# Expert stage of a two-block kernel: plain column halves with eight 64-wide turnings, an earlier position table, a later modulation slot and a split last load

## The reference, cut to what matters

```python
g_p, g_idx = lax.top_k(group_prob, 1)                 # one of 4 groups
e_p, e_idx = lax.top_k(jax.nn.softmax(sel, axis=-1), 2)  # two of its 8 experts
expert = g_idx * EXPERTS_PER_GROUP + e_idx            # 32 experts in all
...
def expert_block(args):                               # xbk: the expert's tokens
    xbk, e = args
    return (jax.nn.silu(xbk @ w_gate[e]) * (xbk @ w_up[e])) @ w_down[e]
...
y = jnp.zeros((N + 1, D)).at[tok_buf].add(yb * w_buf[:, None])
```

## Time and profile before

| | us |
|---|---|
| median of 3 runs | 1467.42 |
| profiled execution | 1468.59 |
| its span | 1466.7 |
| TensorE busy with MATMUL | 1418.4 (97%) |
| first window of expert 0 begins | 256.60 |
| last expert's down product ends | 706.01 |
| one window, from a down product to the next | 13.39 |

### The profile page before, as it was taken

One profiled execution on the slowest core, in us unless ns is written; L12 is line 12 of the kernel. 1 busy time (PEld: TensorE's weight loads), 2 busy tenths in 40 slices (PEclk: granted clock), 3 DMA queues, 4 the chain that ended last, 5 costly groups with the idle time before them and its releaser, 6 DMA issues.

```text
span 1466.7 us, 23746 instructions
## 1 busy us (share of the span) xinstructions
PE 1418.4 (97%) x9490; PEld 930.3 (63%) x9491; DVE 630.2 (43%) x1120; ACT 230.2 (16%) x473; POOL 220.3 (15%) x156
## 2 busy tenths in 40 slices
PE   6999999999999999999999999999999999999997
PEld 4766756654544444444585649998448664999943
DVE  1455646112122222221463425557665472555666
ACT  1320004100000000000312531001031052200001
POOL 2000100000000000000000027770010002677101
PEclk9999999999999999999999999999999999999999
DMA  9954297999999999999999155345428923352610
GB/s 351 330 224 173 91 414 301 368 389 424 417 426 429 427 427 427 428 426 427 407 408 361 69 197 205 117 168 205 172 103 343 379 93 115 104 184 85 232 56 29
DMA packets 91074, 400.92 MB, mean 273 GB/s; under 512 B 7248, under 2 KB 12496, under 8 KB 67824
## 3 DMA queue, kind: packets, MB, share of 16 engines
q1 hardware_dynamic: 90992, 399.73, 69.2%
HBM read 398.66 MB, written 1.05 MB: 273 GB/s over the span
## 4 chain that ended last, share of the span: by engine, by line
PE 88%; DVE 4%; DMA 4%; ACT 1%; issue 1%; SPq 1%; DVEq 0%; ACTq 0%
PE psum L1168 22%; PE psum L1521 17%; PE psum L1573 8%; PE psum L1333 8%; PE psum L1146 4%; PE psum L1483 4%; PE psum L726 3%; DMA ring<-in_moe_up 3%; PE psum L1351 2%; PE psum L1553 2%; PE psum L1366 2%; PE psum L648 1%; DMA ring<-in_ada_w 1%; PE psum L882 1%; PE psum L1114 1%
## 5 line engine op out<-in xcount | busy, mean ns | idle before, releaser
L1168 PE MATMUL psum<-ring,arena 128*64 128x256 f32 (+1 forms) x1728 | 241.1, 433 | 6.1 <-issue 3.8
L1168 PEld LDWEIGHTS psum<-ring,arena 128*64 128x64 f32 x1728 | 123.9, 136 | 126.9 <-issue 70.0
L1521 PE MATMUL psum<-arena,ring 128*128 128x128 f32 x1280 | 150.4, 275 | 2.1 <-ACT arena L2371 2.0
L1521 PEld LDWEIGHTS psum<-arena,ring 128*128 128x128 f32 x1280 | 146.4, 192 | 2.8 <-issue 2.8
L1168 PE MATMUL psum<-arena 128*64 128x256 f32 (+1 forms) x812 | 112.6, 429 | 2.4 <-issue 1.7
L1521 PE MATMUL psum<-arena 128*128 128x128 f32 x960 | 113.7, 275 | 0.0
L1333 PE MATMUL psum<-arena,ring 128*128 128x256 f32 x512 | 112.0, 380 | 1.5 <-DVE arena L1632 1.5
L1521 PEld LDWEIGHTS psum<-arena 128*128 128x128 f32 x960 | 110.4, 192 | 0.0
L1997 DVE TENSOR_TENSOR arena<-psum,arena 128x256 f32<-128x256 f32 x32 | 13.6, 425 | 222.4 <-PE psum L1168 222.4
L1333 PEld LDWEIGHTS psum<-arena,ring 128*128 128x128 f32 x512 | 96.8, 190 | 16.6 <-issue 2.7
L1573 PE MATMUL psum<-arena 128*128 128x512 f32 x220 | 99.3, 593 | 2.1 <-DVE arena L2307 2.1
(11 more groups left out here) (444 smaller groups left out, 1768.8 us busy)
## 6 DMA issues: line engine op xcount, KB each, us to landing
ring<-in_moe_up SPq DMA_DIRECT2D x22, 2048.0 KB, 17.7
ring<-in_moe_down SPq DMA_DIRECT2D x22, 2048.0 KB, 17.1
ring<-in_moe_gate SPq DMA_DIRECT2D x21, 2048.0 KB, 17.5
arena<-in_w_mod SPq DMA_DIRECT2D x32, 1024.0 KB, 8.5
ring<-in_ada_w SPq DMA_DIRECT2D x12, 2048.0 KB, 10.9
ring<-in_w_qkv SPq DMA_DIRECT2D x12, 2048.0 KB, 15.0
arena<-in_moe_gate SPq DMA_DIRECT2D x20, 1024.0 KB, 16.6
arena<-in_moe_up SPq DMA_DIRECT2D x20, 1024.0 KB, 16.2
```

Of the source, the lines that this page charges most:

```text
L1168: ins = mm(bank[b][o, 0:n], lhsT, part_of(w, half), start=first, stop=last, tile_position=(0, 64 * half))
L1521: last = mm(bank[b + k][:, slot * P:slot * P + P], left[:, k, c], right[:, c, :], start=(c == 0), stop=(c == 3))
```

## The change

Seven edits, in the order of the program:

- **Plain columns.** `hidden` is gone: half 0 of gate and up is hidden columns 0 to 255, half 1 is 256 to 511, read without gaps.
- **Turning.** Since the halves lie otherwise, `actm` is turned by eight products with a piece of the identity, each 64x64, in the two column halves of TensorE; their stationary operand is every fourth column of `actm`. `actT` has four chunks of 64 columns.
- **Tokens by chunk.** ScalarE writes the normalized tokens so that the 128 features of a chunk lie side by side; `gather` then reads its stationary operand without gaps, and ScalarE reads its input with a step of 8 elements (L2485 and L2491 of before).
- **Positions.** One of the two `rows` products now stands ahead of the five position products, the other behind; `fill(1)` stands behind both instead of ahead, and the flush behind the first half of `gather`. The ring slot that `fill(1)` reads is freed by the first `gather`, not by the first position product. VectorE's work on the experts' weights stands behind `perm`, and `spread4` behind `mtab`. On ScalarE the modulation copy stands behind the two `gate2b` copies.
- **Loop.** 8 passes in the loop; the ninth is written out, on SyncE and TensorE.
- **Last load.** The last `w_down` comes in two loads of 1 MB, with a semaphore each; TensorE waits for the second ahead of its third chunk.

The diff, cut to its core:

```diff
@@ sync: loads @@
-                at_e = bass.ds(i * PASS + e, 1) if e >= FIRST else slice(e, e + 1)
+                at_e = slice(NE - 1, NE) if last else bass.ds(i * PASS + e, 1) if e >= FIRST else slice(e, e + 1)
+                    if last:
+                        for h in range(2):
+                            sp.dma_start(ring[:, r, 2048 * h:2048 * h + 2048], rows_of[:, h, :])\
+                                .then_inc(S(("once_in", f"slot{r}_loaded")[h == 0]), 16)
+                        return
@@ tensor: between choice and experts @@
-            fill(1)
+            rows(diag[:, 1], 2, 3, parts=(0,))
 
             pe.wait_ge(S("routed"), 4)
-            mm(bank[6][:, 0:NE], upper[:, :], oh[:, 0], start=True, stop=True).then_inc(S("slot_freed"), 1)
+            mm(bank[6][:, 0:NE], upper[:, :], oh[:, 0], start=True, stop=True)
...
-            rows(diag[:, 1], 2, 3)
-            flush()
+            rows(diag[:, 1], 2, 3, parts=(1,))
+            fill(1)
...
-                return mm(gathered(half, c), xr[:, t, :].rearrange("q (p c) -> q c p", c=DC)[:, c, :],
+                return mm(gathered(half, c), xr[:, t, P * c:P * c + P],
                           perm[:, t, TOK * half:TOK * half + TOK], start=(t == 0), stop=(t == 1))
...
-                gather(0, c, 0)
+                ins = gather(0, c, 0)
+                if c == 0:
+                    ins.then_inc(S("slot_freed"), 1)
...
+            flush()
             pe.wait_ge(S("routes_ready"), 1)
@@ tensor: window @@
-                def hidden(w, half):
-                    return w.rearrange("p (q h j) -> p h q j", h=2, j=2)[:, half]
-                def columns(w, half):
-                    return w[:, 512 * half:512 * half + 512]
-                        ins = mm(bank[b][o, 0:n], lhsT, part_of(w, half), start=first, stop=last,
+                        ins = mm(bank[b][o, 0:n], lhsT, w[:, half * n:(half + 1) * n], start=first, stop=last,
                                  tile_position=(0, 64 * half))
...
-                for j in range(2):
-                    last = nc.tensor.transpose(bank[1][:, TOK + j * P:TOK + (j + 1) * P],
-                                               actm.rearrange("p (q j) -> p j q", j=2)[:, j, :], ident[:, :])
+                for k in range(4):
+                    for half in range(2):
+                        hs = slice(64 * half, 64 * half + 64)
+                        last = mm(bank[1][hs, TOK + 64 * k:TOK + 64 * k + 64], actm.rearrange("p (q k) -> p k q", k=4)[:, k, :],
+                                  ident[:, hs], start=True, stop=True, tile_position=(0, 64 * half))
...
-                    last = product(3, actT[:, k % 2, 64 * (k // 2):64 * (k // 2) + 64], w(k), 512, k == 0, k == 3, columns)
+                    last = product(3, actT[:, k, :], w(k), 512, k == 0, k == 3)
...
-            with pe.Fori(0, (NE - FIRST) // PASS, 1) as i:
+            with pe.Fori(0, PASSES - 1, 1) as i:
                 for e in range(FIRST, FIRST + PASS):
                     expert(i, e)
+            for e in range(FIRST, FIRST + PASS):
+                expert(PASSES - 1, e, e == FIRST + PASS - 1)
@@ scalar: normalized tokens, both halves of the tokens @@
-            a_.to(A(xr[:, 0, :], x[:, 0, :], ACT.Copy, scale=stat[:, 2:3]), "h2_ready")
+            a_.to(A(by_chunk(xr[:, 0, :]), x[:, 0, :].rearrange("q (p c) -> q c p", c=DC), ACT.Copy, scale=stat[:, 2:3]), "h2_ready")
```

More of the change, by code:

```diff
@@ L354, in _, with load_matrix @@
             moe_n0 = st_sp.n
-            def load_matrix(i, e, k, halves=(0, 1)):
-                at_e = bass.ds(i * PASS + e, 1) if e >= FIRST else slice(e, e + 1)
+            def load_matrix(i, e, k, halves=(0, 1), last=False):
+                at_e = slice(NE - 1, NE) if last else bass.ds(i * PASS + e, 1) if e >= FIRST else slice(e, e + 1)
                 one = a[("moe_gate", "moe_up", "moe_down")[k]][at_e, :, :]
@@ L403, in _ @@
                 load_matrix(0, *divmod(n, 3))
-            with sp.Fori(0, (NE - FIRST) // PASS, 1) as i:
+            with sp.Fori(0, PASSES - 1, 1) as i:
                 for e in range(FIRST, FIRST + PASS):
@@ L407, in _ @@
                         load_matrix(i, e, k)
+            for e in range(FIRST, FIRST + PASS):
+                for k in range(3):
+                    load_matrix(PASSES - 1, e, k, last=(e == FIRST + PASS - 1 and k == 2))
             st_sp.n += 11 * RING - 1
@@ L1026, in _, with rows @@
                     .then_inc(S("gn_var"), 1)
-            def rows(src, n, b0, freed=None):
+            def rows(src, n, b0, freed=None, parts=(0, 1)):
                 pe.wait_ge(S("diag_ready"), n)
@@ L1031, in rows @@
                     pe.wait_ge(S(freed[0]), freed[1])
-                for k in range(2):
+                for k in parts:
                     mm(bank[b0 + k][:, :], ones[:, :], src[:, 4 * k:4 * k + 4, :], start=True, stop=True)\
@@ L1154, in window, with product @@
             def window(slots, done, frees, copies):
[L1157 to L1165 removed]
+                def product(b, lhsT, w, n, first, last):
                     for half in range(2):
                         o = slice(64 * half, 64 * half + 64)
[L1168 removed]
+                        ins = mm(bank[b][o, 0:n], lhsT, w[:, half * n:(half + 1) * n], start=first, stop=last,
                                  tile_position=(0, 64 * half))
@@ L1197, in window, with expert, second_half @@
                 for k in range(4):
-                    last = product(3, actT[:, k % 2, 64 * (k // 2):64 * (k // 2) + 64], w(k), 512, k == 0, k == 3, columns)
+                    last = product(3, actT[:, k, :], w(k), 512, k == 0, k == 3)
                 last.then_inc(S("down_done"), 1)
-            def expert(i, e):
+            def expert(i, e, last=False):
                 def entry(n):
                     return mtab[0:1, bass.ds(i * PASS + n, 1)] if e >= FIRST else mtab[0:1, n:n + 1]
+                def second_half(w, c):
+                    if c == 2:
+                        pe.wait_ge(S("once_in"), 112)
+                    return w[:, c, :]
                 extra = pe.value_load(entry(NE + e), min_val=0, max_val=3) if e else extra0
@@ L1220, in slots @@
                         w = ring[:, r, :].rearrange("p (c n) -> p c n", c=chunks)
+                        if last and k == 2:
+                            return lambda c: second_half(w, c)
                         return lambda c: w[:, c, :]
@@ L1952, in _ @@
                                                 op0=ALU.is_equal, op1=ALU.add), "perm_ready")
+            dve.wait_ge(S("g_sum"), 2)
+            d(V.reciprocal(gs, gs))
+            dve.wait_ge(S("g_sum"), 3)
+            d(V.tensor_scalar(p1, dd, 1.0, None, ALU.add))
+            d(V.reciprocal(p1, p1))
+            d(V.tensor_tensor(w1, gs, p1, ALU.mult))
             d(V.tensor_tensor(w2, w1, dd, ALU.mult))
-            d.to(V.tensor_tensor(spread4.rearrange("p t k q -> p (t k) q"), ident[:, :].unsqueeze(1).broadcast_to([P, 8, P]),
-                                 vals.rearrange("p t k -> p (t k)").unsqueeze(2).broadcast_to([P, 8, P]), ALU.mult),
-                 "routes_ready")
             dve.wait_ge(S("iota_made"), 2)
@@ L1977, in _ @@
             d.to(V.tensor_copy(mtab[0:1, 2 * NE:3 * NE], pa[0:1, :]), "mtab_ready")
+            d.to(V.tensor_tensor(spread4.rearrange("p t k q -> p (t k) q"), ident[:, :].unsqueeze(1).broadcast_to([P, 8, P]),
+                                 vals.rearrange("p t k -> p (t k)").unsqueeze(2).broadcast_to([P, 8, P]), ALU.mult),
+                 "routes_ready")
             mod_columns()
```

15 lines of the change are left out of this document (6 added, 9 removed).

## The result

The changed kernel takes 1481.73 us (median of five runs, 1476.29 to 1484.91) against 1466.89 for the kernel before: a ratio of 1.0087, with a 95% interval of 1.0065 to 1.0110. It is slower, as forecast, but by 14.8 us where 6.6 were forecast. The profiled execution is the fastest of the five: 1476.29 us with a span of 1474.3. That is 1.1 us over the 1475.2 that the sum gave for a profiled execution; the median is 7.7 us over the forecast of 1474.0 and lies outside the forecast's own range of 1470.3 to 1480. So there are two questions: whether each step holds in the profiled execution, and what the other executions have on top.

The account below looks back on a forecast made before the run. TensorE bounds the expert stage until expert 28, then the loads. From the profiled 1468.59 us: +10.2 windows, -3.5 waits, -0.8 gather, +0.7 stalls = +6.6, so 1475.2, or 1474.0 as median; own range 1470.3 to 1480, 8 in 10 1465.5 to 1484.

Parts of the forecast that it names:

- The bound: Expert stage: TensorE sets the time until expert 28, the loads behind it; longer windows paid nearly in full, 32 times.
- Plain columns, -0.35: Gate and up products: reading columns without gaps saves 0.35 us per window, bounds 0 and 0.5.
- Rival 3: Gate and up: plain columns save nothing, a window grows by 0.67 us, time 1485; chance 0.08.
- The turning, 1.11: Turning of actm in each window: eight products take 1.11 us instead of 0.44, bounds 0.6 and 2.1.
- Rivals 1 and 4: Turning: 1, cheap, kernel faster, 1465.9 at 0.6 us, chance 0.15; 4, halves' loads follow one another, 2.1 us, 1506, chance 0.07.
- rival 1: Turning is cheap and the kernel gets faster; edge at a turning of 0.92 us, 115 ns a pair; chance 0.15.
- Waits for up matrices, -3.5: Last three experts: TensorE's 3.5 us of waits for up matrices go, since TensorE is now the later one.
- Second gather, -0.8: Second half of gather: plain operand saves 0.8 us that counts; the first half's is lost in a pause.
- Positions and loads, 0: Before the first window: it starts at 256.6 as before, within 0.4; two loads some 2.9 us later cost 0.
- Last load in halves, 0: Last down matrix in two loads: gains 0, since the up matrix was what came late.
- Stalls of fresh code, +0.7: Written-out ninth pass: +2.0 for 1.1 stalls of 1.8 us, -1.3 for low clock gone; bounds -6.7 and +7.

Follow-up runs that it names:

- second profile: Profiled execution of a repeat of the unaltered changed kernel, 1482.89 us; that repeat's median was 1482.64 us, ratio 1.0094 to the kernel before.
- window alone: Kernel before with only the plain column halves and the eight 64x64 turnings: 1478.8 us, ratio 1.0081.
- The one with 8 KB pieces: Kernel before with plain gate and up columns, its two transposes kept, down matrix in two 8 KB pieces a partition: 1466.8 us, ratio 0.9998.

## Why the prediction was right, and where it was off

**The bound.** Right. TensorE and the loads are two chains of nearly the same length, and the stage ends with the later. All windows tried show it: 13.71 us and no wait for a matrix; 13.39 and three last windows of some 14.7; 13.05 and eight of 14.8; 12.98 and eleven of 14.9. A longer window is paid 32 times, a shorter one brought nothing in any of the five versions that had one.

**Plain columns, -0.35.** Measured -0.34 (10.83 to 10.49), in every kernel that has them. Rival 3 falls by this. The rule of the Trainium skill (SBUF — State Buffer, the note on cachelines), by which two hits in a line are enough for full bandwidth and nothing would be saved, does not hold exactly for this moving operand (0.34 of 10.83 us are saved). The half of the same note that speaks against the 16-byte step does.

**The turning, 1.11.** Measured 1.10 to 1.11 in every window. The taking apart was right as well: loads side by side, and the step as the price, 214 ns with it and 137 without. Rivals 1 and 4 fall by this row. (The prediction's edge for rival 1, 0.92 us or 115 ns a pair, forgets its own 0.15 for the ends; by its sum the pair would be 96 ns.)

**Waits for up matrices, -3.5.** Gone, as forecast. The 3.5 is right as the length of four windows over four undisturbed ones. Rows 3 have only 1.7 of it as waits; the same view has 0.6 for an up matrix in `arena`, and the rest lies in the products around these waits.

**Second gather, -0.8.** From the first window's turning to the second's it is 22.82 us before and 22.62 after. The window's own +0.32 lies between, so the gather saved 0.5.

**Positions and loads, 0.** Right by the run of this part alone. In the second profile, which has the stretch of low clock at 234 us that the kernel before has, the two loads came 2.6 and 3.1 us later, where 2.9 was forecast (1.2 and 1.7 in the first, which has no such stretch), and cost nothing. ScalarE's gapped copy took 2.17 us, nearly double the 1.15, and that cost nothing either.

**Last load in halves, 0.** Never run by itself; it is within the 0.26% of the written-out pass.

**Stalls of fresh code, +0.7.** This is the term that was off; it was sized too small. In the first profiled execution it was 10.1 - 7.9 = +2.2. In the second, which lies at the median, it was 16.4 - 7.9 = +8.5, which is beyond the bound of +7. The step put it this way: three experts of fresh code bring 1.1 stalls of 1.8 us, and the stretch of low clock goes. In its place the runs show this, each time as window lengths over undisturbed ones. The written-out pass costs 5.3 us in the first profile and 6.9 in the second, where the step had 2.0: its stall is 3.3 us both times, at full length and not 1.8. The front costs 4.8 and 9.5 where the kernel before has 7.9, and the step had 1.3 less than that: its stalls come to 3.8 and 6.8 us, and to 8.3 with the window alone, against 5.4. And the three long stalls of the two profiles each bring a stretch of low clock, which costs 1.4 to 2.8 us (8.56, 8.81 and 9.89 us against 7.13 for the same 64 records); the step counted such a stretch as gone.

Two readings in that step are wrong as well. Counted from 0, as everywhere else, the three stalls of before lie in experts 3, 5 and 7, not 2, 4 and 6. And they begin 20, 16 and 11 records into the gate product, behind the branch at the expert's start, so the branch alone does not put them where the trace has them.

Against the profiled 1468.59 of before, the second profile makes up +10.2 - 3.5 - 0.5 + 8.5 - 0.6 (first window at 255.97) = +14.1, and 1482.89 is +14.3. The first makes up +10.2 - 3.5 - 0.5 + 2.2 - 2.1 (first window at 254.53) = +6.3. It is +7.7, of which 1.0 lies behind the stage, where this execution has a stretch of low clock at 724 us and the kernel before has none. That the forecast for a profiled execution came out within 1.1 us is thus in part luck: the first profile is of the fastest of five executions, with the short second stall. The range for 8 in 10 (1465.5 to 1484) held because it was drawn for the rivals, not for this; the forecast's own range did not hold for the median.

**Open.** Why the packet of code that ends the second stall starts 2.5 us ahead in some executions and 0.5 to 1.3 us late in others, and where the rest of the written-out pass's 3.6 us goes. No version was found that beats the kernel before. The one with 8 KB pieces equals it.

## What to carry to other kernels

Before shortening a loop that runs beside a stream of loads, work out the stream's own time for a pass. If it is the longer one, only the stream is worth work, and a longer loop body is paid in full as soon as the slack is used up. When a step is removed from one operand, look where it reappears: here 0.34 us saved on the moving operand came back as 0.49 on a stationary one. And do not size a term by the one profile at hand if it differs between executions: here that term was +2.2 us in the profile of the fastest execution and +8.5 in that of one at the median.

## What was not expected of the hardware

- Stalls of first-run code are not of one size. With the same program and at the same place they were 0.26 and 3.23 us, and each of the 46 ended 1.2 to 1.9 us after a 16 KB packet of the instruction queue had landed. Between 280 and 380 us that queue moves 0.16 to 0.20 MB in the three kernels looked at (before, changed, window alone); the amount does not tell them apart, the start of the packet does.
- The rule of the Trainium skill (Runtime: NRT & Kernel Launch, "Instruction fetch mechanics"), that a taken branch to a page not at hand waits for its fetch, fits the stalls at 336 and 686 us of the second profile, which begin where an expert and its branch begin. The other two begin 15 and 23 records behind that, and the section gives no size.
- Loads from memory in pieces of 4 KB a partition on a third of the bytes brought the stream from 427 to 421 GB/s, 8 KB to 425 or 426. Where the stream sets the end this decides: 1.4% of 450 us is 6 us.
- Two products of 256 columns side by side take 0.216 us with a plain moving operand, 0.227 with pairs in every four columns.
- A low clock while the experts are chosen (0.66 over 25 us) came in two of fourteen profiles, in kernels with the old and the new order of positions, and moved the first window by 6 us.
